# Six expert places refilled as one ring, with the down weights issued from a second DMA queue

## What is computed

```python
for l in range(2):
    sh1, sc1, g1, sh2, sc2, g2 = silu(cond) @ ada_w[l] + ada_b[l]   # six parts of 1024
    x = x + g1 * mixer_l(rms_norm(x) * (1 + sc1) + sh1)
    h = rms_norm(x) * (1 + sc2) + sh2
    # top expert group of 4, top 2 of its 8 experts; combine[t, e] is 0 for the others
    hid = silu(h @ w_gate[e]) * (h @ w_up[e]) * combine[:, e]       # 1024 -> 256
    x = x + g2 * sum_e(hid @ w_down[e])                             # 256 -> 1024
```

## Time and profile before

| | us |
|---|---|
| median of 3 runs | 882.83 (878.4 to 884.16) |
| the profiled execution | 882.42 |
| its span, first to last instruction | 880.3 |
| PE busy | 731.0 (83%) |
| expert stage, layer 0: first `gate_up` to last `down` | 284.4 to 532.5 |
| expert stage, layer 1 | 617.2 to 853.1 |

### The profile page before, as it was taken

How to read it: one execution, slowest core, us unless ns; L and a number is a source line. 1 busy time by engine, 2 the same in 40 slices (tenths; PEclk the granted TensorE clock), 3 DMA queues, 4 the chain that set the end, 5 groups by cost and what they waited for, 6 DMA issues and landing times.

```text
span 880.3 us, 12828 instructions
## 1 busy us (share of the span) xinstructions
PE 731.0 (83%) x4560; PEld 404.0 (46%) x4560; DVE 352.0 (40%) x830; ACT 141.5 (16%) x342; POOL 175.7 (20%) x275
## 2 busy tenths in 40 slices
PE   4899989999985999998778871966999997888860
PEld 3333433468744555544434430735555553444430
DVE  2212548642254344443332334555244443333333
ACT  3111154531351000000000002543000000000000
POOL 0000400000002133343223220001143433332220
PEclk9999999999895999999999987885899999999995
DMA  9999849841859879999999955975688999999935
GB/s 348 427 436 411 220 147 419 310 188 68 360 190 340 294 311 399 421 420 419 419 420 424 419 211 191 425 296 180 241 361 335 418 423 423 421 423 421 421 158 215
DMA packets 39525, 294.32 MB, mean 334 GB/s; under 512 B 10600, under 2 KB 12064, under 8 KB 19520
## 3 DMA queue, kind: packets, MB, share of 16 engines
q1 hardware_dynamic: 26800, 275.51, 76.9%
q0 software_dynamic: 10880, 13.26, 4.9%
q10 hardware_dynamic: 1808, 5.06, 1.4%
HBM read 293.24 MB, written 22.02 MB: 358 GB/s over the span
## 4 chain that ended last, share of the span: by engine, by line
PE 54%; DMA 36%; DVE 4%; issue 2%; ACT 2%; SPq 1%; POOL 0%; POOLq 0%; DVEq 0%; ACTq 0%
DMA ring<-in_moe_w_in 25%; PE bank L1572 17%; PE bank L1316 7%; PE bank L1596 6%; PE bank L1241 4%; PE bank L1415 3%; DMA ring<-in_ada_w 3%; DMA ring<-in_moe_w_out 3%; PE bank L1546 2%; DMA adaw<-rows,gidx 2%; DMA adaw<-results 2%; PE bank L1423 2%; PE bank L1458 2%; PE bank L1375 1%; DMA rows<-qkv 1%
## 5 line engine op out<-in xcount | busy, mean ns | idle before, releaser
L1572 PE MATMUL bank<-ring,qkv 128*64 128x256 f32 x1952 | 240.3, 401 | 47.9 <-DMA ring<-in_moe_w_in 22.5
L1572 PEld LDWEIGHTS bank<-ring,qkv 128*64 128x64 f32 x1952 | 150.3, 144 | 119.9 <-issue 44.0
L1096 DVE COPY qkv<-bank 128x512 f32<-128x512 f32 x64 | 44.3, 692 | 212.3 <-PE bank L1546 212.3
L537 POOL DMA_INDIRECT results<-adaw,scur x65 | 67.8, 1043 | 297.1 <-DVE adaw L1119 260.0
L1596 PE MATMUL bank<-ring,qkv 128*64 128x512 f32 x488 | 118.1, 604 | 1.1 <-DVE qkv L1108 0.8
L795 ACT ACTIVATE qkv<-bank 128x128 f32<-128x128 f32 x64 | 17.8, 278 | 460.0 <-PE bank L1572 460.0
L527 POOL DMA_INDIRECT adaw<-rows,gcur x57 | 59.2, 1039 | 44.3 <-POOL gcur L524 44.3
L1316 PE MATMUL bank<-ring,hT 128*128 128x512 f32 x144 | 65.2, 608 | 1.3 <-DVE hT L869 1.3
L1546 PE MATMUL bank<-con,adaw 128*128 128x128 f32 x260 | 43.5, 291 | 11.8 <-DMA adaw<-rows,gidx 9.9
L1596 PEld LDWEIGHTS bank<-ring,qkv 128*64 128x64 f32 x488 | 30.0, 136 | 46.0 <-issue 44.1
L1117 DVE SCALAR_TENSOR_TENSOR adaw<-qkv,wcur 128x512 f32<-128x512 f32 x64 | 48.1, 752 | 2.3
(11 more groups left out here) (236 smaller groups left out, 721.9 us busy)
## 6 DMA issues: line engine op xcount, KB each, us to landing
ring<-in_moe_w_in SPq DMA_DIRECT2D x61, 2048.0 KB, 22.7
ring<-in_moe_w_out SPq DMA_DIRECT2D x61, 1024.0 KB, 22.0
adaw<-in_ada_w SPq DMA_DIRECT2D x15, 2048.0 KB, 10.4
ring<-in_ada_w SPq DMA_DIRECT2D x9, 2048.0 KB, 10.6
ring<-in_attn_w_qkv SPq DMA_DIRECT2D x3, 2048.0 KB, 36.0
ring<-in_attn_w_o SPq DMA_DIRECT2D x1, 4096.0 KB, 21.4
adaw<-in_moe_w_in SPq DMA_DIRECT2D x2, 2048.0 KB, 26.5
adaw<-results SPq DMA_DIRECT2D x8, 512.0 KB, 6.4
```

Source lines behind the costliest of these rows:

```text
L537: pool.indirect_dma_start(res, bass.IndirectOffsetOnAxis(ap=scur[:, p, :], axis=0), yout[:, p], None, bounds_check=res_limit, oob_is_err=F ...
L1096: V.tensor_copy(xgT[:, p], bank[2][:, :]).then_inc(xgT_ready, 1)
L1572: last = T.matmul(bank[p][64 * a:64 * a + 64, 0:2 * P], xk[:, k % 4, k // 4], w[k // IN_X if b > RING else 0][:, k % IN_X if b > RING else ...
```

## The change

- All six places form one ring (`SLOTS = 6`): expert s goes into place s % 6, for the whole layer, and its refill waits for expert s - 6.
- The refills of gates are issued by SyncE, with `gu_mm` as their only wait. The refills of downs are issued by ScalarE, between two `silu`, after `down_mm`. Place 4 takes its downs in two DMAs, place 5 its gates in two.
- TensorE's loop body grows from 4 to 12 steps, so that place, buffer and count can be written out.
- Layer 0: the last two ada chunks (22 and 23) both go to `adaw[:, 0]`. Chunk 23 is issued after `more_gu` instead of at the end of the attention, and can only be issued when `ada(22)` is through. In return expert 3's downs and the second half of its gates are issued before expert 0, and the first half right after expert 2.
- Layer 0: `vectors(3)` moves behind the second table product (line 1525), and VectorE takes its result between two row copies of the expert stage. Layer 1: `keep(4)` and `keep(5)` (line 1509) go ahead of the first table product.
- The extra tile's expert goes into place 2 after `down` of expert 26.

```diff
-        ADA_AT = [TAIL, LEFT, RIGHT, HIGH0, HIGH1] + [(i + 2) % 3 for i in range(5, 2 * NCH)]
+        ADA_AT = [TAIL, LEFT, RIGHT, HIGH0, HIGH1] + [(i + 2) % 3 for i in range(5, 2 * NCH - 2)] + [LEFT, LEFT]
...
-            for i in range(8, 2 * NCH):
+            for i in range(8, 2 * NCH - 1):
                 load_ada(i)
...
                 if l == 0:
+                    load_out(sp, l, 3, 3, s_wout[3])
+                    sp.dma_start(ring[:, 3, KD * FE:2 * KD * FE], moe_w_in[l, 3, :, KD * FE:2 * KD * FE]).then_inc(s_win[3], 16)
                     sp.wait_ge(pv_mm, NU // 4)
                     for b in range(2):
                         load_expert(l, b)
                     sp.wait_ge(mix_mm[0], 2 * KD)
                     load_expert(l, 2)
-                    sp.wait_ge(ada_mm, 23)
-                    load_expert(l, 3)
+                    sp.dma_start(ring[:, 3, 0:KD * FE], moe_w_in[l, 3, :, 0:KD * FE]).then_inc(s_win[3], 16)
                     sp.wait_ge(ada_vec, 2)
+                    sp.wait_ge(ada_mm, 22)
...
-                sp.dma_start(more_gu, moe_w_in[l, RING]).then_inc(s_more, 16)
+                load_in(l, RING, RING, s_win[RING])
+                if l == 0:
+                    load_ada(2 * NCH - 1)
                 sp.wait_ge(hb_mm, l * 6 + 6)
...
-                def refill(s, b):
-
-                    refill_in(s, b, RING)
-                    refill_out(s - 1, (b - 1) % RING, RING)
...
+                for s in range(SLOTS, SLOTS + 2):
+                    refill_in(s, s - SLOTS)
+                first = SLOTS + 2
+                loops = (NE - first) // SLOTS
                 with sp.Fori(0, loops) as r:
+                    for b in range(SLOTS):
+                        refill_in(r * SLOTS + (first + b), (first + b) % SLOTS)
...
                 def load_extra(j):
                     e = sp.value_load(extra_e[0:1, bass.ds(j, 1)], min_val=0, max_val=NE - 1)
-                    sp.wait_ge(down_mm, l * NE + LAST[EXTRA_SLOT] + 1)
+                    sp.wait_ge(down_mm, l * NE + LAST_OF_EXTRA_SLOT + 1)
...
+                def refill_out(s, b):
+                    act.wait_ge(down_mm, s + (l * NE + 1 - SLOTS))
+                    load_out(act, l, s, b, s_wout[b])
+
                 silu(0, 0, old=False)
...
                 with act.Fori(0, loops) as r:
+                    for b in range(first, first + SLOTS):
+                        silu(r * SLOTS + b, b % 2)
+                        refill_out(r * SLOTS + (b + SLOTS - 1), (b - 1) % SLOTS)
...
-                for n in range(4):
+                for n in range(6 if l else 4):
                     keep(n)
...
                 if l == 0:
-                    vectors(3)
-
-                keep(4)
-                keep(5)
+                    keep(4)
+                    keep(5)
...
                 last.then_inc(tab_mm, 1)
+                if l == 0:
+                    vectors(3)
```

More of the change, by code:

```diff
@@ L293, in build @@
         s_rowsout = sem("s_rowsout")
[L295 to L301, removed]
+        s_win = [sem(f"s_win{b}") for b in range(SLOTS)]
+        s_wout = [sem(f"s_wout{b}") for b in range(SLOTS)]
+        WIN_DMAS = [16] * RING + [16, 32]
+        WOUT_DMAS = [16] * RING + [32, 16]
+        PER_LAYER = [len(range(b, NE, SLOTS)) for b in range(SLOTS)]
+        EXTRA_SLOT = NE % SLOTS
+        LAST_OF_EXTRA_SLOT = NE - SLOTS
         s_xg = [sem(f"s_xg{b}") for b in range(NBUF)]
@@ L366, in build, with load_out @@
         block = ctx.enter_context(nc.Block())
+        def load_out(eng, l, e, b, arrived):
+            w = moe_w_out[l, bass.ds(e, 1)].rearrange("o p n -> (o p) n")
+            if b < RING:
+                eng.dma_start(ring[:, b, 2 * KD * FE:], w).then_inc(arrived, 16)
+            elif b == RING:
+                for j in range(2):
+                    eng.dma_start(more_down[j], w[:, j * D:(j + 1) * D]).then_inc(arrived, 16)
+            else:
+                eng.dma_start(sixth_down, w).then_inc(arrived, 16)
         @block.sync
@@ L432, in _ @@
                 sp.wait_ge(x1_mm, l * 6 + 6)
-                for part, a, b in ((sixth_gu[0], 0, IN_X), (sixth_gu[1], IN_X, KD)):
-                    sp.dma_start(part, moe_w_in[l, RING + 1, :, a * 2 * FE:b * 2 * FE]).then_inc(s_six, 16)
+                load_in(l, RING + 1, RING + 1, s_win[RING + 1])
                 sp.wait_ge(xg_mm, l * NE + 1)
-                sp.dma_start(sixth_down, moe_w_out[l, RING + 1]).then_inc(s_six_out, 16)
-                def refill_in(s, b, old):
-                    sp.wait_ge(gu_mm, s + (l * NE + 1 - old))
+                load_out(sp, l, RING + 1, RING + 1, s_wout[RING + 1])
@@ L440, in refill_in @@
+                def refill_in(s, b):
+                    sp.wait_ge(gu_mm, s + (l * NE + 1 - SLOTS))
                     load_in(l, s, b, s_win[b])
[L442 to L454 removed]
@@ L455, in _ @@
-                refill_in(AHEAD + RING, 0, RING)
-                refill_out(AHEAD + RING - 1, RING - 1, AHEAD)
-                first = AHEAD + RING + 1
-                loops = (NE - first) // RING
-                with sp.Fori(0, loops) as r:
-                    for b in range(RING):
-                        refill(r * RING + (first + b), (b + 1) % RING)
-                for s in range(first + RING * loops, NE):
-                    refill(s, (s - 2) % RING)
-                refill_out(NE - 1, (NE - 3) % RING, RING)
+                for s in range(SLOTS, SLOTS + 2):
+                    refill_in(s, s - SLOTS)
@@ L795, in silu @@
                     A.activation(gated[:, p], bank[p][:, 0:P], ACT.Silu).then_inc(silu_ready, 1)
+                def refill_out(s, b):
+                    act.wait_ge(down_mm, s + (l * NE + 1 - SLOTS))
+                    load_out(act, l, s, b, s_wout[b])
                 silu(0, 0, old=False)
-                for s in range(1, RING + 2):
-                    silu(s, s % 2, old=s > 1)
-                loops = (NE - RING - 2) // 2
+                silu(1, 1, old=False)
+                refill_out(SLOTS, 0)
+                first, last = 2, NE - SLOTS + 1
+                loops = (last - first) // SLOTS
                 with act.Fori(0, loops) as r:
-                    for b in range(2):
-                        silu(r * 2 + (RING + 2 + b), b)
+                    for b in range(first, first + SLOTS):
+                        silu(r * SLOTS + b, b % 2)
+                        refill_out(r * SLOTS + (b + SLOTS - 1), (b - 1) % SLOTS)
+                for s in range(first + SLOTS * loops, NE):
+                    silu(s, s % 2)
+                    if s < last:
+                        refill_out(s + SLOTS - 1, (s - 1) % SLOTS)
                 act.wait_ge(x_down[l], 1)
@@ L1122, in experts @@
                 rows_T(0, 0, old=False)
+                if l == 0:
+                    dve.wait_ge(ada_vec, 4)
+                    modulation(2, 0, 5, 6)
+                    modulation(2, 1, 0, 6)
+                    V.memset(ss[:, 17:18], 0.0).then_inc(mods_ready, 1)
                 rows_T(1, 1, old=False)
```

78 lines of the change are left out of this document (35 added, 43 removed).

## The result

The changed kernel takes 901.04 us (median of 4 runs, 898.12 to 906.11); the kernel before, run beside it, takes 881.59 (4 runs, 878.40 to 884.16). The ratio is 1.0227, 95% interval 1.0183 to 1.0272. The forecast was 877, with a range of 867 to 890: the time lies outside it, on the other side.

The account below looks back on a forecast made before the run. The prediction took DMA standstills to set the end of the expert stages; layer 0 (-5.3 + 3 + 4 = +1.7) and layer 1 (-1 - 6.6 + 0 = -7.6) gave -5.9 on 882.42, so 876.5, shown as 877, range 867 to 890.

Parts of the forecast that it names:

- What bounds the kernel: Both expert stages: they begin at TensorE's pace (6.32 us an expert), end at the DMA's (8.1); DMA standstills count.
- The gap of experts 4 and 5: Mid expert stage, DMA idle because places 4 and 5 weren't refilled; six-place ring gains 5.3 us (layer 0), 6.6 (layer 1).
- Two queues: 0 in themselves: Expert refills: splitting gates and downs over two queues adds no bandwidth; they share two to one, 0 us.
- ScalarE's issue costs nothing: Between two silu in the expert stages: a down refill's issue takes 0.33 us, covered by waiting; 0 us.
- Start of layer 0, +3: Before layer 0's experts: chunk 23 lands later, delaying routing and first gather; stream starts some 3 us late, bounds +1 to +6.
- Start of layer 1, -1: Before layer 1's experts: sixth_gu goes about 3 us earlier, out of the first gather's way; -1 us, bounds 0 and -3.
- End of layer 0, +4: Last downs land with the extra tile's weights, exposing 5.3 us of work hidden before; +4 us, bounds 0 and 5.3.
- End of layer 1, 0: After the last gates: about as much transfer, 4.9 us, stays behind them if both queues keep step; 0, bound +4.9.
- Downs run ahead, gates late: Rival, expert stages: engines favour the down queue, gates come late, no change, about 884 us; chance 0.18.
- the down queue starves: Rival, expert stages: place 4's 4 KB down rows need too many turns, TensorE waits for downs; 895 us, chance 0.15.

Follow-up runs that it names:

- e1_one_queue: Changed kernel with the down refills issued by SyncE again, so one hardware queue, six-place ring kept: 870.23 us, ratio 0.9838 to the kernel before.
- e6_half_turns: Changed kernel, two hardware queues kept, every row of an expert's load halved (gates 8 KB, downs 4 KB): 884.26 us, ratio 1.0026.
- e8_downs_4k: Changed kernel with the downs of all places in rows of 4 KB, gates still in 16 KB: 897.01 us, ratio 1.0151.
- e3_small_turns: Changed kernel, two queues, with the gates of places 0 to 4 loaded in two DMAs with rows of 8 KB instead of 16 KB: 883.38 us, ratio 1.0021.
- e9_more_scatters: e1_one_queue plus two more GpSimd scatters per tile, 256 bytes of each row, into tensors nobody reads: 880.74 us, ratio 0.9979.
- e10_empty_scatters: e9_more_scatters with all row numbers of the added scatters out of bounds, so they write nothing: 880.79 us, ratio 0.9978.

## Why the prediction was wrong, step by step

**What bounds the kernel: right for the kernel before, and this set the trap.** It said that only the moments at which the DMA stands still count. The changed kernel's DMA doesn't stand still, carries its weights about as fast as any, and is 20 us slower.

**The gap of experts 4 and 5, -5.3 and -6.6: right.** e1_one_queue's stages are 5.2 and 6.1 us shorter than before, and in the kernel after the share is 1.02 from 320 to 330, where it was 0.34 from 322 to 330.

**"Two queues: 0 in themselves": the step that failed.** Its words were "the queues take turns row by row", which the packet counts bear out, and it worked out what turns do to gates and downs. It left out the third queue in the circle. The numbers for it stood in the profile of before: the page's row of the software queue with its 10880 packets, 10400 of them for 130 gathers and scatters, which the prediction didn't use, and 420 GB/s over 16 engines, which makes 0.62 us for a row of 16 KB and 0.31 for one of 8. That gives 10 turns of 0.93 us, 9.3 us for what must be done in 6.32. (The expectations of e6_half_turns and e8_downs_4k say 10.5 turns, with all 10880 packets spread over the 130.) Measured is +10.8 and +9.0 us over before in the two stages, +16.0 and +15.1 over e1_one_queue. The rule of the Trainium skill that the prediction weighed ("DMA: Bandwidth & Descriptors", section "Issuing engines are not separate DMA queues") holds for bandwidth: 413 GB/s with two queues, 412 with one. It does not speak of latency there, and the loss was in latency.

**ScalarE's issue costs nothing: right for this change, but it has a condition that was not named.** In the kernel after an issue took 0.34 us. In e6_half_turns and e8_downs_4k, with 104 DMAs of weights in ScalarE's queue instead of 60, single issues took up to 6.8 and 12.9 us, and silu came late behind them.

**Start of layer 0, +3: right**, +3.1 in ScalarE's timeline, +3.03 at the first `gate_up`, and about +3.2 over all kernels when counted from `ada(22)`. Chunk 23 landed at 252.19 + 12.62 = 264.8, for which 263.6 was said.

**Start of layer 1, -1: right in sign**; from the extra tile to the first silu of layer 1 there are 3.0 us less, which was the bound. The first gather holds the chain for less than the 6 us that were hoped for, where it had 7.31; which part of the rest comes from elsewhere was not looked into.

```profile
618.64 3.70 DMA adaw<-rows,gidx
```

**End of layer 0, +4: wrong, -3.8.** It took the last downs for late. But weights came before they were needed, since TensorE was behind: no wait for a DMA stands ahead of the extra `gate_up`. A step that rests on the DMA being the bound falls with it.

**End of layer 1, 0:** -0.3, right, though for the reason just given and not for its own.

**The rivals.** "Downs run ahead, gates late" and "the down queue starves" were not what happened, but each is what happens once the sizes of the rows are changed (e3_small_turns, e8_downs_4k). The rival that was missing is a gather that is served too seldom: its price, as measured, is some 10 us a layer over the kernel before.

## What to carry to other kernels

Moving part of a stream to a second DMA queue adds no bandwidth, but puts another row into each turn of every DMA engine; whoever has many small packets in a third queue pays for it in latency. Here that made 901 us of 870. Count the packets of each operation and multiply by the time of one row of each busy queue, and compare with the pace of the loop. If two large streams must go side by side, short rows kept the gathers in time here; but keep the ratio of the rows at the ratio of the bytes that are needed, and issue them from an engine that has nothing else to do, since long issues held silu (a kernel with all three was not built). And a test that adds DMAs adds the work of issuing them: look at the issuer's timeline before the loss is put down to the DMA engines.

## What the runs showed of the hardware

- With three queues full, the DMA engines began 95, 94 and 97 packets of them in 5 us, and 660, 658 and 664 in 35 us: equal numbers, whether of 16 KB (615 ns), 8 KB (309 ns) or 8 bytes (9 ns).
- A gather or scatter of 128 row numbers with 2 KB each has 80 packets, two row numbers to a packet. A scatter of 256 bytes a row has 32, and as many when all its row numbers are out of bounds (14976 packets in both e9_more_scatters and e10_empty_scatters).
- An issue of a DMA took 0.34 us in the kernel after, and up to 6.8, 12.9 and 11.2 us in e6_half_turns and e8_downs_4k (on ScalarE) and e1_one_queue (on SyncE). How much a queue takes before that was not measured.
- GpSimd needed 6.6 to 7.3 us to issue four indirect DMAs with what goes between them, more than TensorE's step of 6.32.
- Two pieces of 4 KB that lie side by side were carried as one row of 8 KB (10448 packets, as with one piece).
